# Two fused transformer blocks on one core: the modulation pieces leave the expert stage, and the mixers' output projection runs column half by column half

## The reference

```
h = x
for layer in range(2):                      # block 1
    xn = rms_norm(h, norm1_g[layer])
    proj = xn @ w_in[layer]                 # 9 groups of 512 columns
    mix  = retention(...) ++ hgrn2(...)     # 512 + 512 columns
    h = h + mix @ w_out[layer]              # 1024 x 1024
    xn = rms_norm(h, norm2_g[layer])
    affinity = softmax(xn @ w_router[layer])          # 256 x 16
    gate, idx = top_k(affinity.T, 32)                 # 16 experts x 32 tokens
    for e in range(16):                               # three 1024 x 1024 weights each
        ye = (silu(xe @ w_gate[e]) * (xe @ w_up[e])) @ w_down[e] * gate
    h = h + scatter(ye)
x = rms_norm(h, final_norm_g)
for i in range(2):                          # block 2: latent x and context ctx
    m = silu(c) @ w_ada[i] + b_ada[i]       # 6144 columns: sh1 sc1 gt1 sh2 sc2 gt2; c_ctx alike
    x = x + gt1 * norm(mixer(modulate(norm(x), sh1, sc1)))     # i=0 pooling, i=1 attention
    x = x + gt2 * norm(sq_relu_mlp(modulate(norm(x), sh2, sc2)))
    # i=0 does the same for ctx
```

## Time and profile before

| | |
|---|---|
| device time, 3 runs | median 2110.59 us (2109.51 to 2112.42) |
| the profiled execution | 2113.23 us, span of its instructions 2110.9 us |
| busy: TensorE, VectorE, ScalarE | 1744.7, 796.9, 520.8 us |
| TensorE's mean granted clock | 0.91 |
| DMA | 629.10 MB, 298 GB/s on average |
| longest share of the chain that ended last | TensorE 57%, DMA 32% |

### The profile page before, as it was taken

The page is one execution under the profiler, slowest core; times in us unless marked ns, Lnnn a source line. Parts: engine busy times, 40 slices in busy tenths (PEclk is TensorE's granted clock), DMA queues, the critical chain, the costliest instruction groups (busy, mean ns, idle before and its releaser), DMA issues.

```text
span 2110.9 us, 25989 instructions
## 1 busy us (share of the span) xinstructions
PE 1744.7 (83%) x10876; PEld 1150.9 (55%) x10876; DVE 796.9 (38%) x1175; ACT 520.8 (25%) x778; POOL 36.4 (2%) x42
## 2 busy tenths in 40 slices
PE   6998767678898849997677898866778999998998
PEld 5876423343454328875334354432247996457887
DVE  6594301211111026764201111121046676555766
ACT  5633110200000025432010000011144343343433
POOL 0000000000000000000000000000010000000000
PEclk9999778889999979998788999997889999998999
DMA  7475699999999993574899999999963454304451
GB/s 268 157 265 201 264 421 421 429 423 423 424 421 424 425 405 136 204 267 195 344 420 423 423 425 422 424 425 421 427 233 146 168 191 159 120 1 159 173 186 60
DMA packets 124799, 629.10 MB, mean 298 GB/s; under 512 B 5024, under 2 KB 7200, under 8 KB 99744
## 3 DMA queue, kind: packets, MB, share of 16 engines
q1 hardware_dynamic: 122000, 616.58, 72.9%
q0 software_dynamic: 2272, 9.44, 1.1%
q10 hardware_dynamic: 432, 1.70, 0.2%
HBM read 624.56 MB, written 3.15 MB: 297 GB/s over the span
## 4 chain that ended last, share of the span: by engine, by line
PE 57%; DMA 32%; DVE 5%; ACT 4%; issue 1%; SPq 0%; POOL 0%; DVEq 0%; ACTq 0%
DMA ring<-in_w_up 18%; PE bank L525 9%; PE bank L527 9%; PE bank L526 9%; PE bank L851 7%; DMA ring<-in_w_mlp_in 6%; PE bank L981 5%; PE bank L999 4%; DMA ring<-in_w_mlp_out 4%; PE bank L1194 2%; PE bank L537 2%; DMA ring<-in_w_in 1%; DVE w_low L425 1%; PE bank L1294 1%; ACT w_high L425 1%
## 5 line engine op out<-in xcount | busy, mean ns | idle before, releaser
L851 PE MATMUL bank<-ring,xeT 128*32 128x512 f32 x1984 | 285.2, 724 | 131.8 <-DMA ring<-in_w_up 131.5
L851 PEld LDWEIGHTS bank<-ring,xeT 128*32 128x32 f32 x1984 | 73.1, 124 | 333.1 <-issue 333.0
L425 ACT ACTIVATE silu_g<-bank 128x256 f32<-128x256 f32 x32 | 12.3, 384 | 741.7 <-PE bank L851 741.7
L425 DVE TENSOR_TENSOR hid_e<-silu_g,bank 128x256 f32<-128x256 f32 x32 | 13.5, 421 | 411.7 <-ACT silu_g L425 411.7
L525 PE MATMUL bank<-x_high,w_high 128*128 128x256 f32 x512 | 147.5, 288 | 11.0 <-DVE x_low L425 5.9
L2308 DVE TENSOR_TENSOR w_low<-ring,w_high 128x1024 fp32r<-128x1024 f32 x128 | 151.9, 1219 | 9.3 <-POOL y L425 4.9
L886 PE MATMUL bank<-ring,hid_T 128*32 128x256 f32 x2048 | 124.9, 390 | 29.9 <-DMA ring<-in_w_down 23.6
L981 PE MATMUL bank<-ctx_xT,ring 128*128 128x256 f32 x512 | 128.1, 417 | 25.7 <-DMA ring<-in_w_mlp_in 25.7
L1657 ACT ACTIVATE w_high<-ring 128x1024 fp32r<-128x1024 f32 x128 | 128.0, 1050 | 86.0 <-PE bank L527 86.0
L527 PE MATMUL bank<-x_high,w_low 128*128 128x256 f32 x512 | 146.4, 286 | 0.0
L526 PE MATMUL bank<-x_low,w_high 128*128 128x256 f32 x512 | 146.3, 286 | 0.0
(11 more groups left out here) (275 smaller groups left out, 2630.9 us busy)
## 6 DMA issues: line engine op xcount, KB each, us to landing
ring<-in_w_down SPq DMA_DIRECT2D x64, 2048.0 KB, 25.5
ring<-in_w_gate SPq DMA_DIRECT2D x62, 2048.0 KB, 20.1
ring<-in_w_up SPq DMA_DIRECT2D x62, 2048.0 KB, 22.9
ring<-in_w_ada SPq DMA_DIRECT2D x24, 2048.0 KB, 9.9
ring<-in_w_mlp_in SPq DMA_DIRECT2D x24, 2048.0 KB, 8.6
ring<-in_w_mlp_out SPq DMA_DIRECT2D x24, 2048.0 KB, 7.9
ring<-in_w_in SPq DMA_DIRECT2D x18, 2048.0 KB, 9.1
ring<-in_w_out SPq DMA_DIRECT2D x4, 2048.0 KB, 8.1
```

The lines of the kernel that those rows point to most:

```text
L425: self.ins, self.mine = op(*args, **kw), "none"
L851: ins = mm(ps[32 * j:32 * j + 32, :], xeT[:, g % 2, c, i * CAP:(i + 1) * CAP], w[:, :, k, j, :, :], start=c == 0, stop=c == KC - 1, skip_g ...
```

## The change

- Pieces of `w_ada` are placed anew. Layer 0's early six are its pieces 0 to 5 as before; then four (`ADA_REST`, pieces 6 to 9) around the output projection and router. Layer 1's mixer uses pieces 10, 11 of layer 0 and 0 to 3 of layer 1; around its output projection 4, 5, 10, 11. The last four (6 to 9 of layer 1, `ADA_LAST`) are used in block 2's attention. No piece is left among the experts.
- The output projection runs n outermost (half 0 for both row tiles, then half 1). After half 0 the slot of its weights and the high buffer that it used come free, after half 1 the other two.
- The router's transposes take `h` itself, not the normalised rows; row tile 0's transposes and logits stand inside the last product (`amid`), and 1/rms is applied in the exponential's scale.
- At the mixer's end, `high_item(OUT_1)` and `low_item(OUT_1)` move behind the normalisation; retention rows are gated and scaled in place; the second row tile's statistics no longer hold up the first. In the conversion, ScalarE writes all high chunks and VectorE each low chunk straight from PSUM in one operation.
- `root_table()` is a 128x1 square root that brings its table in ahead of the statistics. At the start, the first weight comes as two 1 MB halves, and the tables and masks are queued behind it on SyncE's queue; only the identity comes first.

```
-LATE_AFTER = [{0: late[2:4], 1: late[4:6]} for late in ADA_LATE]
-MOE_SLOTS = (6, 7, 4, 5, 0, 1, 2, 3)
+ADA_EARLY = (pieces(0, 0, 6), pieces(0, 10, 12) + pieces(1, 0, 4))
+ADA_REST = (pieces(0, 6, 10), pieces(1, 4, 6) + pieces(1, 10, 12))
+ADA_LAST = pieces(1, 6, 10)
...
+        for piece, slot in zip(ADA_REST[layer], (b, d)):
+            item(("ada", *piece), slot, 1)
+        rounded = [4 + (SPLITS * layer + j) % 2 for j in (OUT_0, OUT_1)]
         for n in range(2):
             item(("w_out", layer, n), (c, a)[n], 1)
-        count[2][4:6] = [count[0]] * 2
+            count[2][rounded[n]] = count[0]
+        for piece, slot in zip(ADA_REST[layer][2:], (b, d)):
+            item(("ada", *piece), slot, 1)
+        slots = itertools.chain((6, 7), itertools.cycle((rounded[0], c, rounded[1], a, b, d)))
...
             ret_out()
+            early_columns(len(ADA_EARLY[l]) - 1)
             hgrn_out()
...
             transposes(("mix", l), lambda t: xs[:, t, :], mix_ready)
+            rest_ada(0)
+
+            def turn_rows(t):
...
+                for b in range(2):
+                    name = ("x2", l, t, b)
+                    ps = take(pe, name, 4 + 2 * t + b)
+                    for c in range(4):
+                        ins = turn(ps[:, c * P:(c + 1) * P],
+                                   h[:, t, :].rearrange("p (n c) -> p c n", c=KC)[:, 4 * b + c, :],
+                                   ident)
+                    fill(ins, name)
...
+            amid = {3: lambda: turn_rows(0), 7: lambda: logits(0)}
+            for n in range(2):
+                for t in range(NT):
...
+                    if n == 0:
+                        rest_columns(t)
+                        if t == 0:
+                            rest_ada(1)
...
+            turn_rows(1)
+            rest_ada(2)
+            logits(1)
+            rest_columns(2)
             pe.wait_ge(S_("affinity_ready"), NT * (l + 1))
...
+            rest_ada(3)
+            rest_columns(3)
...
-                for n in LATE_AFTER[l].get(e, ()):
-                    late_ada(n)
...
+        ada_item(ADA_LAST[0], 1)
         turn_tile(0)
...
+                if (t, n) == (0, 0):
+                    last_columns(0, 1)
...
+        ada_item(ADA_LAST[1], 6)
         pe.wait_ge(S_("q_rot_ready"), NT)
...
+        last_columns(1, 6)
+        ada_item(ADA_LAST[2], 5)
         pe.wait_ge(S_("k_rot_ready"), NT)
...
+        last_columns(2, 5)
+        ada_item(ADA_LAST[3], 6)
...
         scores(0)
         scores(1)
+        last_columns(3, 6)
...
+                ins = stt(xT_low[:, c, :].rearrange("p (t n) -> p t n", t=NT),
+                          ps[:, at_:at_ + S].rearrange("p (t n) -> p t n", t=NT), gain(c),
+                          xs_high[:, :, c, :].bitcast(F32), ALU.mult, ALU.subtract)
...
+                free(f(logit[:, t, :], ps[:, 0:NEXP], ACT.Exp, scale=rinv[:, t:t + 1],
+                       bias=rstats[:, t, 1:2], accum_out=rstats[:, t, 2:3]), name)
```

More of the change, by code:

```diff
@@ L335, in build_program, with block2_first @@
                 item(("ctx", CTX_MID[layer][e]), next(slots), 1)
-            for n in LATE_AFTER[layer].get(e, ()):
-                item(("late", layer, n), next(slots), 1)
+    def block2_first(layer):
+        if layer == 0:
+            return [("mix2", 0, 0)]
+        last = [("ada", *piece) for piece in ADA_LAST]
+        return (last[:1] + [("mix2", 1, n) for n in range(3)] + last[1:]
+                + [("mix2", 1, n) for n in (3, 4)])
     order2 = sorted(range(RING2), key=lambda slot: count[2][slot])
@@ new lines, in logits @@
+            def logits(t):
+                for b in range(2):
+                    freed(pe, ("x2", l, t, b))
+                name = ("logit", l, t)
+                ps = take(pe, name, 4 + t)
+                pe.wait_ge(S_("router_landed"), 16 * (l + 1))
+                for c in range(KC):
+                    ins = mm(ps[:, 0:NEXP], xT[:, c, t * P:(t + 1) * P], wr[:, c, :],
+                             start=c == 0, stop=c == KC - 1)
+                fill(ins, name)
+            amid = {3: lambda: turn_rows(0), 7: lambda: logits(0)}
@@ L1339, in odd_chunks, with root_table @@
                 free(ins, (tag, b))
+        def root_table():
+            step(f(spare[:, :], eps[:, :], ACT.Sqrt))
         def high_chunks(tag, gain):
-            for b in (1, 3):
+            for b in range(4):
                 ps = full(act, (tag, b))
@@ new lines, in split_chunks, with ada_bias @@
+                free(ins, (tag, b))
+                after(b)
+        def ada_bias(tag, batch):
+            ps = full(dve, tag)
+            runs = []
+            for k, (layer, n) in enumerate(batch):
+                if runs and runs[-1][0] == layer and runs[-1][1] + runs[-1][3] == n:
+                    runs[-1][3] += 1
+                else:
+                    runs.append([layer, n, k, 1])
+            for layer, n, k, some in runs:
+                ins = tt(mods[:, layer, 4 * n:4 * (n + some), :],
+                         ps[:, 8 * k:8 * (k + some)].rearrange("p (a b) -> p a b", b=2),
+                         C("b_ada", NMOD * KC * layer + 4 * n, 4 * some).unsqueeze(2)
+                         .broadcast_to([P, 4 * some, 2]), ALU.add)
+                if k + some < len(batch):
+                    tick(ins)
+            free(ins, tag)
@@ L1844, in lower_bounds, with gains @@
+        def gains(layer, which, pre):
+            at_ = (3 * which + 1) * KC
+            for s in range(2):
+                tick(stt(mod_gain[:, layer, which, s, :], mods[:, layer, at_:at_ + KC, s], 1.0,
+                         C(pre, KC * layer, KC), ALU.add, ALU.mult))
         def lower_bounds():
```

384 lines of the change are left out of this document (191 added, 193 removed).

## The result

The changed kernel takes 2028.18 us, median of 4 runs (2026.49 to 2028.84), beside 2110.05 (2104.61 to 2112.42, 4 runs) for the kernel before on the same chip: ratio 0.9614, 95% interval 0.9595 to 0.9634. Direction and main term held; the size did not. They ran on three chips, so small differences in us are read with the ratios beside them.

What follows compares the result with a forecast made beforehand. Experts bound by bytes over rate at 422 GB/s, the rest by chains of small waits. From 2113.2 us, -39.8 - 8 - 10 - 4 + 5 = -56.8 gives 2056.4, less 2.6: 2054 us; range 2040 to 2072.

Steps and rivals of the forecast that it cites:

- Term 1: Expert stages: with the pieces gone, four 2 MB items fewer per layer at 4.97 us each, -39.8 us.
- Term 2: Kernel start: smaller loads ahead and early tables let TensorE begin at 15.8 instead of 22.77, -8 us.
- Term 3: Mixer end to router affinities: earlier transposes and projection, router work inside the last product, -10 us over both layers.
- Term 4: Beginnings after the experts (layer 1's start, before block 2): table load off the path, first weight sooner, -4 us.
- Term 5: Block 2's attention: the four pieces and columns placed there only partly fit in TensorE's waits, +5 us.
- A: Experts: TensorE becomes the bound and half of term 1 is lost, 2074 us; chance 0.12.
- B: Output projection: its insertions aren't paid back, terms 3 and 4 give nothing, 2068 us; chance 0.13.
- E: Experts: the stream is limited otherwise than by its bytes, four items fewer save nothing, 2094 us; chance 0.03.
- D: Context turns: TensorE falls to 1.2 GHz, 11 us more per turn, slower, up to 2230 us; chance 0.02.
- C: Router: TensorE's clock stays up through spread and gather, 2045 us; chance 0.17.

Runs made afterwards that it cites:

- b2_before_warm: The kernel before, with 40 unread identity multiplications filling TensorE's wait at the mixer's end: 2104.65 us, ratio 0.9980.
- r2_items_front: The changed kernel with both halves of the second output weight back in front of ScalarE's squares and VectorE's gating: 2040.72 us.
- r3_router_after: The changed kernel with nothing inside the last product; row tile 0's transposes and logits follow it: 2040.21 us.
- t1_no_tables: The changed kernel without the 128x1 roots and exponential that bring a table in ahead of its use: 2039.16 us.
- m1_in_turns: The changed kernel with its last four pieces moved from block 2's attention back among layer 1's experts: 2047.15 us.
- w2_warm_waits: The changed kernel with unread identity multiplications only where TensorE waits around the router's last columns, top-8, spread and gather: 2024.43 us.
- a0_after_again: The changed kernel unchanged, run a second time as the base of the experiments: 2028.91 us.

## Why the prediction was wrong, step by step

**Term 1 held.** 39.8 forecast, 42.3 and 39.7 in two pairs of traces, and 20.5 for four items between two runs that differ in these pieces alone.

**Term 2 held**: first product at 15.8 as forecast, fifth chunk without a wait.

**Term 3 is the step that failed**: "mixer end to affinities: -10 us over both layers", measured -22 and -21. The mechanism was right and the sum too small. In layer 1 of the first pair the forecast is 6.1 us short, by its own steps:

- The transposes begin 4.7 earlier relative to the mixer (forecast 4.6).
- I then had 6.2 us to the projection's start, because I priced transposes and piece toward the low clock ("or, at half the clock, up to 3.6"); it is 4.7 (5.1 and 5.3 in the second trace).
- I added 7.6 us to the projection's 24.0; it grew by 5.0. The clock is only part of it: in the traces of before the two projections take 23.6 to 25.5, with the wait filled 23.6 in both layers, so 0.4 here and 1.9 in the second pair. The larger part is the price of the inserted work. I had added up the lengths of rows, 7.1. But a row's length reaches into the next one, and the row of logits that I had halved (4.46) ran partly at the low clock: the half takes 1.93 now. The five insertions put off the next matmul by 6.1, and the logits waited for nothing, where I had 0.5. That leaves 0.7 of the 2.6 open.
- From its end to the affinities I had 9.0, it is 8.1, and from there to expert 0 it takes another 1.0 less, the gather running partly at the full clock.

The columns of one piece inside the projection: their row has 0.95, and the next row starts 0.88 behind theirs.

```profile
911.78 0.95 PE L555 MATMUL bank<-consts_sb,ada_rows 128*128 128x2 f32 x8
912.66 1.92 PE L540 MATMUL bank<-ring,silu_c 128*32 128x512 f32 x16
914.51 0.50 PE L527 MATMUL bank<-w_high,xs_high 128*128 128x512 f32 x1
```

I read the 0.77 matmul of the earlier trace rows as the price of a start, not as the clock. That the clock falls in the wait and can be kept up is shown by `b2_before_warm`; that the parts were worth more than I had priced, by `r2_items_front` (11.8 where the sum had 9) and `r3_router_after` (11.3 where it had 8.6). How much of the term the clock makes up changes from one execution to the next, and for layer 0 (5.9 and 3.4 short) I have not taken it apart.

**Term 4 was too small.** Layer 1's start gave 2.7 and its fifth chunk's wait (1.35) went, 4.1 against 3.3. Block 2's head, from the last down to its first MLP, gave 2.8 and 3.8 against 0.8. The table load is 1.3 of it. The rest is in rows that I had not looked at. VectorE and GpSimd in that place, second trace of before, and then the changed kernel:

```profile
1547.35 2.30 DVE L425 SCALAR_TENSOR_TENSOR x<-h,rinv,final_g_row 128x1024 f32<-128x1024 f32 x1
1549.95 1.28 DVE L425 SCALAR_TENSOR_TENSOR x<-h,rinv,final_g_row 128x1024 f32<-128x1024 f32 x1
1551.54 0.75 DVE L425 TENSOR_SCALAR xs<-x,rinv 128x1024 f32<-128x1024 f32 x1
1552.97 2.24 DVE L425 TENSOR_SCALAR xs<-x,rinv 128x1024 f32<-128x1024 f32 x1
1546.67 1.90 POOL L425 TENSOR_TENSOR diag<-consts_sb,gate_col 128x1024 f32<-128x1024 f32 x1
1552.77 1.89 POOL L425 TENSOR_TENSOR diag<-consts_sb,gate_col 128x1024 f32<-128x1024 f32 x1
```

```profile
1469.33 1.29 DVE L435 SCALAR_TENSOR_TENSOR x<-h,rinv,final_g_row 128x1024 f32<-128x1024 f32 x1
1470.92 2.81 DVE L435 SCALAR_TENSOR_TENSOR x<-h,rinv,final_g_row 128x1024 f32<-128x1024 f32 x1
1470.76 1.89 POOL L435 TENSOR_TENSOR diag<-consts_sb,gate_col 128x1024 f32<-128x1024 f32 x1
```

The same operation takes 1.28 us alone and 2.30 or 2.81 while GpSimd builds `diag`; before there were two such meetings ahead of the pooling, after one. `t1_no_tables` bears it out: with the table load back in the path this stretch takes 46.1 us as it did before (46.4), against 43.6 and 42.5 in the changed kernel, and both meetings are back (2.34 and 2.28 us). So the load moved VectorE's rows into GpSimd's and cost more than its own 1.3. No run here moved GpSimd's work alone.

**Term 5 was nearly right**, 5 forecast, 3.3 measured between the two kernels. Columns +1.0, ahead of k +1.1 (1.4), ahead of the scores +2.0 (1.9). But behind that it gave 0.9 back instead of costing 1: the pieces fill the waits, and the scores run at 2.4 GHz. The same clock again.

**Not in the sum at all**: 5 us in the MLPs, of which the 32 bytes account for 3.2 to 4.5. And I took off 2.6 us for the profiled execution being long; against the second trace of before it was 5.4 long. The account, then: term 3 is 11 to 12 of the 26 us missed, MLPs 5, block 2's head 2 to 3, attention 2, layer 1's start 1, and the remaining 4 I put down to the first trace of before, which also had the longer waits in the mixers.

**The rivals.** A, B and E are out by `m1_in_turns` and `r3_router_after`. D did not come: the clock in the context turns is 0.93 to 0.95 as before. C as I stated it (spread under 2.5 us) did not come either, 3.77 in both layers; it needed the fill of `w2_warm_waits`. My error was to see the clock as a rival at `spread` alone, and not at the transposes, the projection and the scores, where the change shortens or fills the wait ahead.

## What to carry to other kernels

A wait of TensorE can cost twice: itself, and the half clock of what follows; so price each shortened or filled wait with the rows behind it at both speeds, and try filling what can't be shortened. Price inserted work by how far it puts off the next row's start, not by its row's length. Work that a stream can hide belongs where the stream has room, and its price is bytes over rate as long as the DMA share is 1. And a new tile in the middle of the allocations is part of a change: measure it alone before crediting the rest.

## What was not expected of the hardware

- The place of tiles in SBUF: with the tiles behind `spare` 32 bytes lower, so that the activations that the MLPs' matmuls read begin on odd multiples of 32 bytes, an MLP iteration takes 45.50 us, and 45.09 with them on even ones, the instructions being the same (a 128x512 matmul 396 and 394 ns).
- 40 unread multiplications that outlast their wait by 1.5 us still make the way from first transpose to projection 1.7 us shorter, and the kernel before no slower (0.9980).
- ScalarE's table load: the next instruction starts 1.30 us after the load's start. The Trainium skill, "ScalarE: Activation LUTs", section "What ACT_TABLE_LOAD costs", adds a drain of 1.38 us; by that page's 2.66 us for each of seven loads I estimate 19 us for `t1_no_tables`. It cost 10.3, with all that the loads set off, and the measurement decides.
- VectorE and GpSimd hold each other up: VectorE's 1.28 us becomes 2.30 and 2.81, and in `a0_after_again` GpSimd's `diag` takes 2.83 instead of 1.89. The Trainium skill, "SBUF — State Buffer", section "SBUF: two separate sides", tells of a port pair that one of the two takes for a whole instruction while the other is blocked. The rows agree: GpSimd's `diag` ends at 1472.65, and VectorE's operation, begun at 1470.92, ends 1.1 us behind it, where it takes 1.29 alone.
